# Expert blocks of 32 rows in quarter rows instead of 64 rows in half rows, in a fused encoder layer with a two-level mixture of experts

## What is computed

```python
g_sel = jnp.argmax(g_logits, axis=-1)                 # 1 of 4 groups
top_v, top_j = lax.top_k(e_logits, TOP_K)             # 2 of its 8 experts
gates = p_g[:, None] * jax.nn.softmax(top_v, axis=-1)
expert_idx = g_sel[:, None] * EXPERTS_PER_GROUP + top_j
...
def expert_block(args):
    x_b, e = args
    hid = jax.nn.silu(x_b @ w_gate[e]) * (x_b @ w_up[e])   # 1024 -> 512
    return hid @ w_down[e]                                 # 512 -> 1024
...
y = jnp.einsum('tkd,tk->td', y_assign, gates)
x = x + y ; final RMSNorm
```

## Time and profile before

| | us |
|---|---|
| device time, median of 3 runs | 866.73 |
| the 3 runs | 861.77, 866.73, 867.14 |
| the profiled execution, from its first to its last instruction (span) | 864.3 |
| PE busy in it | 831.4 (96%) |
| DVE / ACT / POOL busy | 418.5 / 215.9 / 140.0 |
| bytes moved by DMA | 261.95 MB, 303 GB/s over the span |

### The profile page before, as it was taken

One profiled execution on the slowest core, in us unless ns is written; L12 is line 12 of the kernel. 1 busy time (PEld: TensorE's weight loads), 2 busy tenths in 40 slices (PEclk: granted clock), 3 DMA queues, 4 the chain that ended last, 5 costly groups with the idle time before them and its releaser, 6 DMA issues.

```text
span 864.3 us, 15988 instructions
## 1 busy us (share of the span) xinstructions
PE 831.4 (96%) x5906; PEld 563.8 (65%) x5907; DVE 418.5 (48%) x825; ACT 215.9 (25%) x461; POOL 140.0 (16%) x279
## 2 busy tenths in 40 slices
PE   7999999999999999799999999999999999999995
PEld 5888988777877888665555555555555555555541
DVE  4699999986564535563222222222222222222237
ACT  3423211557875333101110011110111101111013
POOL 3300010000000011112222212222122222122101
PEclk9999999999999999899999999999999999999999
DMA  7353645131253198889999999999999999999998
GB/s 198 79 137 101 184 180 178 58 87 36 75 166 128 69 412 314 349 345 406 420 417 418 377 405 419 417 421 418 420 418 420 422 419 420 420 419 421 419 387 322
DMA packets 81143, 261.95 MB, mean 303 GB/s; under 512 B 19274, under 2 KB 45130, under 8 KB 56523
## 3 DMA queue, kind: packets, MB, share of 16 engines
q1 hardware_dynamic: 63392, 240.92, 71.3%
q0 software_dynamic: 7888, 18.78, 5.6%
q10 hardware_dynamic: 9818, 1.66, 1.0%
HBM read 246.49 MB, written 24.20 MB: 313 GB/s over the span
## 4 chain that ended last, share of the span: by engine, by line
PE 81%; DVE 12%; DMA 3%; issue 2%; SPq 1%; ACT 1%; POOL 0%; POOLq 0%; DVEq 0%; ACTq 0%
PE ps L1490 30%; PE ps L1536 16%; PE ps L1214 9%; PE ps L1350 8%; DVE big L1968 7%; PE ps L1504 3%; PE ps L1428 3%; PE ps L1266 2%; PE ps L1233 2%; DMA big<-results 2%; PE ps L1245 1%; PE ps L1493 1%; DVE w_split L1905 1%; DMA big<-h_rows,idx_of 1%; PE ps L1173 1%
## 5 line engine op out<-in xcount | busy, mean ns | idle before, releaser
L1493 PE MATMUL ps<-ring,big 128*64 128x256 f32 x688 | 153.9, 382 | 0.2 <-DMA ring<-in_w_up 0.2
L1490 PE MATMUL ps<-ring,big 128*64 128x256 f32 x672 | 150.3, 382 | 1.2 <-issue 1.2
L1214 PE MATMUL ps<-hT,w_split 128*128 128x256 f32 (+1 forms) x744 | 136.9, 341 | 0.0
L1490 PEld LDWEIGHTS ps<-ring,big 128*64 128x64 f32 x672 | 92.5, 138 | 56.7 <-issue 13.5
L1830 ACT ACTIVATE big<-ps 64x256 f32<-64x256 f32 x78 | 29.3, 376 | 392.5 <-PE ps L1493 341.6
L1214 PEld LDWEIGHTS ps<-hT,w_split 128*128 128x128 f32 x744 | 113.5, 190 | 20.5 <-issue 7.0
L2301 DVE TENSOR_TENSOR big<-ps,big 64x256 f32<-64x256 f32 x78 | 33.2, 426 | 182.5 <-ACT big L1830 155.1
L1490 PE MATMUL ps<-big 128*64 128x256 f32 x544 | 120.2, 379 | 0.0
L1493 PE MATMUL ps<-big 128*64 128x256 f32 x544 | 120.2, 379 | 0.0
L1490 PEld LDWEIGHTS ps<-big 128*64 128x64 f32 x544 | 74.5, 137 | 46.5 <-issue 9.7
L1493 PEld LDWEIGHTS ps<-ring,big 128*64 128x64 f32 x688 | 94.7, 138 | 1.7 <-DMA ring<-in_w_up 0.7
(11 more groups left out here) (298 smaller groups left out, 1197.4 us busy)
## 6 DMA issues: line engine op xcount, KB each, us to landing
ring<-in_w_down SPq DMA_DIRECT2D x44, 1024.0 KB
ring<-in_w_up SPq DMA_DIRECT2D x43, 1024.0 KB, 15.1
ring<-in_w_gate SPq DMA_DIRECT2D x42, 1024.0 KB
big<-in_w_gate SPq DMA_DIRECT2D x20, 1024.0 KB, 7.2
big<-in_w_up SPq DMA_DIRECT2D x20, 1024.0 KB
big<-in_w_down SPq DMA_DIRECT2D x20, 1024.0 KB
w_raw<-in_w_in SPq DMA_DIRECT2D x20, 512.0 KB, 3.8
results<-spare POOLq DMA_DIRECT2D x12, 512.0 KB, 3.3
```

Source lines behind the costliest of these rows:

```text
L1214: mm = pe.matmul(ps[:, n % 2, 0:size], w_split[:, sub, hi_w, k, :], hT[:, k // 4, hi_h, k % 4, cols], **flags)
L1490: pe.matmul(ps[0:BLK, 6 * h, 0:FH], xT[:, k, q, :], gate[2][:, k, fs], **flags)
L1493: mm = pe.matmul(ps[BLK:2 * BLK, 6 * h + 1, 0:FH], xT[:, k, q, :], up[2][:, k, fs], **flags)
```

## The change

`BLK` becomes 32 and a token row is kept as four quarter rows of 256 (`QS` = 4), so that a block of 32 tokens again fills 128 partitions. The scratch tensors have four rows for each token, and the indices sent to the indirect DMAs count quarter rows. A token's one-hot has 32 columns, so that four products (instead of two) put it on the four quarters of the partitions. `MAXN` becomes 24 and `NB` 82, and the buffers of a block are packed anew.

On PE, `gate_up` still makes two passes over the hidden columns (h), but a pass has four column groups of 32: two for gate and two for up, each with 128 moving columns. All four write one PSUM bank. Down has four groups of 32 with 256 columns each. The transposes become products with parts of the identity, 64 moving columns for the rows and 32 for the hidden halves, and `turn_hidden(b, 1)` moves behind the first quarter of down (k = 0). The last block's result, two quarters for each partition half, is scattered into half rows by DVE before `late` uses it. The loads of weights, their pieces, their waits and the table `PLACES` stay as they are.

```diff
-BLK = 64
+BLK = 32
+QS = P // BLK
...
-    h_rows = nc.dram_tensor("h_rows", (2 * T, D // 2), F32, kind="Internal").ap()
-    results = nc.dram_tensor("results", (4 * T, D // 2), F32, kind="Internal").ap()
+    h_rows = nc.dram_tensor("h_rows", (QS * T, D // QS), F32, kind="Internal").ap()
+    results = nc.dram_tensor("results", (2 * QS * T, D // QS), F32, kind="Internal").ap()
...
             def turn_rows(rows=xb):
                 for k in range(KD // 2):
-                    mm = pe.transpose(ps[:, 4, k * P:(k + 1) * P], rows[:, k:HD:KD // 2], ident[:])
+                    for e in range(2):
+                        mm = pe.matmul(ps[64 * e:64 * e + 64, 4, 2 * BLK * k:2 * BLK * (k + 1)], rows[:, k:QD:KD // 2],
+                                       ident[:].rearrange("p (q e n) -> p e q n", q=2, e=2)[:, e], start=True, stop=True)
...
-                    for half in range(2):
-                        mm = pe.matmul(ps[half * BLK:(half + 1) * BLK, 3, 0:NB], row_hot[:, a, :], block_hot[:, a, :],
+                    for s in range(QS):
+                        mm = pe.matmul(ps[s * BLK:(s + 1) * BLK, 3, 0:NB], row_hot[:, a, :], block_hot[:, a, :],
                                        start=(a == 0), stop=(a == 2 * NT - 1))
...
                 for k in range(KD // 2):
                     flags = dict(start=(q == 0 and k == 0), stop=(q == 1 and k == KD // 2 - 1))
-                    if h == 0 and k == 0:
-                        pe.wait_ge(gate[0], gate[1])
-                    pe.matmul(ps[0:BLK, 6 * h, 0:FH], xT[:, k, q, :], gate[2][:, k, fs], **flags)
-                    if h == 0 and k == 0:
-                        pe.wait_ge(up[0], up[1])
-                    mm = pe.matmul(ps[BLK:2 * BLK, 6 * h + 1, 0:FH], xT[:, k, q, :], up[2][:, k, fs], **flags)
+                    for a, (landed, target, w) in enumerate((gate, up)):
+                        if h == 0 and k == 0:
+                            pe.wait_ge(landed, target)
+                        for c in range(2):
+                            at, cols = (2 * a + c) * BLK, (2 * h + c) * P
+                            mm = pe.matmul(ps[at:at + BLK, 6 * h, 0:P], xT[:, k, q, :], w[:, k, cols:cols + P], **flags)
...
                 for k in range(KF // 2):
-                    mm = pe.transpose(ps[:, 5 * (1 - h), k * BLK:(k + 1) * BLK],
-                                      hb[:, h * FH + k:(h + 1) * FH:2], ident[0:BLK, 0:BLK])
+                    for c in range(2):
+                        mm = pe.matmul(ps[64 * c:64 * c + 64, 5 * (1 - h), k * BLK:(k + 1) * BLK],
+                                       hb[:, h * P + k:(h + 1) * P:2], ident[0:2 * BLK, c * BLK:(c + 1) * BLK], start=True, stop=True)
...
                 turn_rows()
-                turn_hidden(b, 1)
...
-                    pe.matmul(ps[0:BLK, 2, :], hbT[:, k, :], down_w[s][:, k, 0:512], start=(k == 0), stop=(k == KF - 1))
-                    mm = pe.matmul(ps[BLK:2 * BLK, 2, :], hbT[:, k, :], down_w[s][:, k, 512:1024],
-                                   start=(k == 0), stop=(k == KF - 1))
+                    if k == 1:
+                        turn_hidden(b, 1)
+                    for c in range(QS):
+                        mm = pe.matmul(ps[c * BLK:(c + 1) * BLK, 2, 0:QD], hbT[:, k, :], down_w[s][:, k, c * QD:(c + 1) * QD],
+                                       start=(k == 0), stop=(k == KF - 1))
...
-                    nc.scalar.activation(sG[:, h * FH:(h + 1) * FH], ps[0:BLK, 6 * h, 0:FH], ACT.Silu).then_inc(sg_ready[h], 1)
+                    nc.scalar.activation(sG[:, h * P:(h + 1) * P], ps[0:2 * BLK, 6 * h, 0:P], ACT.Silu).then_inc(sg_ready[h], 1)
...
-                nc.vector.tensor_tensor(hb[:, fs], ps[BLK:2 * BLK, 6 * h + 1, 0:FH], sG[:, fs],
+                nc.vector.tensor_tensor(hb[:, fs], ps[2 * BLK:4 * BLK, 6 * h, 0:P], sG[:, fs],
                                         ALU.mult).then_inc(hb_ready[h], 1)
...
-            result(last, 1, pairs + 2, late_y)
+            dve.wait_ge(base_ready, last + 1)
+            dve.wait_ge(y_done, last + 1)
+            V.scalar_tensor_tensor(late_rows[:, 0:QD], ps[:, 2, 0:QD], late_scales[:, 0, 0:1], late_rows[:, 0:QD], ALU.mult, ALU.add)
+            V.scalar_tensor_tensor(late_rows[:, QD:2 * QD], ps[:, 2, 0:QD], late_scales[:, 1, 0:1], late_rows[:, QD:2 * QD],
+                                   ALU.mult, ALU.add).then_inc(late_y, 1)
```

More of the change, by code:

```diff
@@ L1472, in rows_and_gates @@
                 for a in range(2 * NT):
-                    for half in range(2):
-                        pe.matmul(ps[half * BLK:(half + 1) * BLK, 5, 0:NB], row_hot[:, a, :], gates_block[:, a, :],
+                    for s in range(QS):
+                        pe.matmul(ps[s * BLK:(s + 1) * BLK, 5, 0:NB], row_hot[:, a, :], gates_block[:, a, :],
                                   start=(a == 0), stop=(a == 2 * NT - 1))
@@ L1477, in rows_and_gates @@
                 for t in range(NT):
[L1478 to L1479 removed]
+                    for s in range(QS):
+                        mm = pe.matmul(ps[s * BLK:(s + 1) * BLK, 5, NB:2 * NB], row_hot[:, t, :], root_block[:, t, :],
                                        start=(t == 0), stop=(t == NT - 1))
@@ L1577, in late @@
                 for half in range(2):
-                    own = slice(half * BLK, (half + 1) * BLK)
-                    mm = pe.matmul(ps[:, LATE_BANK[t] + half, :], late_hot[own, t, :], yb2[1][own, :], start=True, stop=last)
+                    own = slice(half * P // 2, (half + 1) * P // 2)
+                    mm = pe.matmul(ps[:, LATE_BANK[t] + half, :], late_hot[own, t, :], late_rows[own, :], start=True, stop=last)
                 return mm
@@ L2306, in hidden, with result @@
                     hidden_half(b, h)
-            def result(b, q, stored, evacuated=y_evac):
+            def result(b, q, stored):
                 dve.wait_ge(base_ready, b + 1)
```

110 lines of the change are left out of this document (65 added, 45 removed).

## The result

| | before | after |
|---|---|---|
| device time, median us | 866.93 (4 runs, 861.77 to 868.34) | 922.59 (4 runs, 918.3 to 923.09) |
| span of the profiled execution, us | 864.3 | 920.5 |
| PE busy, us | 831.4 | 837.1 |

The ratio is 1.0645, with a 95% interval of 1.0607 to 1.0682: 6.5% slower, outside the forecast range of 868 to 899. The direction was right, the size was not: 16.6 us were forecast and 56 came.

A forecast was written before the change was run, and what follows sets the result against it. PE and DMA were both taken as bounds. With PE late, the last weights were to land at 852.6, 16.6 us later than before; added to the median of 866.7 that gave 883.3 us, range 868 to 899.

The forecast's parts named there:

- the two bounds 3 us apart: In the kernel before, PE's chain of blocks and the DMA queue of weights both bind, ending within 3 us of each other.
- The frame of the sum: Late PE: last weights land at 500.2 + 47 P + 22 B, plus 0.6, so 852.6; the tail of 28.3 follows.
- P: PE's time for one block of 32 tokens after the change: 6.97 us, bounds 6.1 and 7.4.
- B: PE's uncovered step from one expert to the next, with two table loads: about 1.1 us, bounds 0 and 1.5.
- some 5 us sooner: At the start of the blocks, block 0 runs this much sooner, so its six pieces are issued by 374.7 us.
- a sign of being wrong: Ahead of 366 us, before the expert blocks: the span growing there by more than 1 us; about 0.4 was expected.
- 16 products for the rows at 0.029: PE's turn of the next block's rows, priced at 0.46 us a block within P.
- the sequencer is held until the second hidden half is ready: At an expert's end, PE's sequencer then has only the last 8 short groups, 0.86 us, to cover its 2.0 us.
- its cover: The first four down products hide the second hidden turn's wait; without them the next late thing costs about 0.3 us.
- The idle stretch near 390 us: DMA engines idle from 387.5 to about 395 us, until block 2 releases its slots: 7.6 us lost.
- Rows in quarters: Half as large pieces on the software DMA queue cost 0 to 9 us more; 3 us taken.
- rival 3: Four column groups on PE don't run at once, so P is 12.0 and the time about 1,145 us; chance 0.02.

The follow-up runs named there:

- runs 6 and 7: The kernel before with the turn of the next block's rows issued twice (881.81 us, ratio 1.0174), and with one of its four transposes (865.67 us, ratio 0.9988).
- run 5: The changed kernel without any load of weights after the first three slots and the lent pieces are filled: 895.63 us, ratio 1.033.
- runs 11 and 14: The changed kernel with the row turn's 64 stationary columns side by side instead of every fourth one, on two chips: 938.25 and 941.4 us.
- run 1: The changed kernel with most of the turn of the next block's rows left out (k = 0 only): 888.09 us, ratio 1.0268.
- run 2: The changed kernel with the second hidden turn back ahead of down: 909.2 us, ratio 1.0508.
- run 3: The changed kernel reading the first block from the table once per loop turn, adding the count for the other two experts: 915.85 us, ratio 1.0567.
- runs 1 to 5, 8 to 10 and 16 to 18: The changed kernel itself or with edits to row turn, hidden turn, table reads, loop places, late weights or result stores: from 883.39 to 922.12 us.

## Why the prediction was wrong in size

- **The bound before** and the two bounds 3 us apart: right, by runs 6 and 7.
- **The frame of the sum** (landing = end of place 1 + blocks x P + steps x B + the last 36 pieces + a tail of 28.3) was right: from the end of place 23 at 797.8 to the last weights are 94.2 us, where the formula has 94.4 with the measured P, and the tail is 28.5. Three terms put into it were not. The landing was to be at 852.6 and was at 892.0, 39.4 later.
- **The failed step, first part: a term that is missing.** The chain from block 0 on priced PE's instructions and not their arrival. The code of a block doubled in products, and late code cost up to 20.6 us (against run 5): 7.3 ahead of the end of place 1 (404.6 measured, 397.3 in run 5 without weights), 13.3 after it. The forecast had place 1 end at 399.1, so 5.5 of the miss lie there. Against run 5 that figure is 1.8 us too late, and so it hid a part of the error by luck; the prediction's own 391.2 + 6.97 give 398.2, and the other 0.9 has no source in it. Nor did block 0 end "some 5 us sooner": it ended 2.5 sooner, as it started 1.1 later (367.15 against 366.01, just over what the prediction named as a sign of being wrong) and its gate/up took 6.2 us, at a granted clock of 0.50 in 365 to 370 us and 0.77 in 370 to 375. No row of the kernel before warns of late code: its gap of 1.18 us between the row numbers and block 1 has no fetch in the 13 us ahead of it.
- **The failed step, second part: P was 7.34, not 6.97.** Gate/up, 3.50 us of products (32 x 0.109) against 3.58, down 1.72 as forecast, and the change of shape 0.13 each against 0.15 were right. The sizing "16 products for the rows at 0.029" was wrong: they start in pairs 0.12 us apart, 0.060 a product, 0.96 us instead of 0.46. The 0.029 came from the earlier trace rows, products of the same shape whose stationary columns stand side by side; here they stand four apart, and runs 11 and 14 show that this is the difference. The right row stood in the earlier trace rows: the transposes of 128 x 128 with the same spread columns start 0.12 apart (four in 0.72 with a change of shape). All in all 0.37 x 47 = 17.4 us. The mechanism, PE's period, was right by run 1.
- **Third: B was 1.26 on average, not 1.1.** The mechanism, "the sequencer is held until the second hidden half is ready", is shown by run 2, and the reading of the table by run 3. In the loop two ends of three cost 1.19; the third, where the loop turns, has a second branch and costs 1.59, which I didn't count. 3.5 us.
- 5.5 + 13.3 + 17.4 + 3.5 is 39.7, against the 39.4.
- **The cost of the move.** I priced the second hidden turn's new place at a change of shape of 0.15, and its cover at 0.3. It was 0.14 and, by run 2, 13 us for the kernel in all; the cover was not needed, since with the turn back in its place no wait for DVE or ACT shows from 500 to 780 us. At the new place it was the loads of down that waited for ACT, 0.2 us a block.
- **The idle stretch near 390 us** was forecast as 7.6 us from 387.5 and is 12, because block 2 starts at 397.3 instead of 391.2: the late code again.
- **Rows in quarters** were taken at 3 us. From 500 to 860 us the software queue takes 6.7% of 360 x 16 us for 9.13 MB, 42.3 ns a kilobyte, as before: nothing. So no run shows the 3 us, nor the 0.6 of them in the sum.
- **Four groups overlap** (against rival 3): four products of 128 columns start 0.007 us apart and the next four 0.109 after them (read at 578.6 us).

## What to carry to other kernels

A bound that doesn't change (here 192 pieces of 1 MiB) caps what any cut of the other bound can give; ask first what the halved unit does to the number of units (39 to 62) and to what is paid once for each, such as turns of rows, changes of shape and reading a table. Count instructions as well as their time: twice the instructions per block is twice the code, and code that is run for the first time while DMA is full can arrive late. The sequencer's lead is a resource of its own: a wait moved nearer to the end of a loop body takes it away, and whatever the sequencer does between two loops is then exposed. A product's price is to be taken from a row with the same spacing of its stationary columns, not only the same shape.

## What the runs showed of the hardware that was not expected

- Code fetched beside full DMA queues delays PE by up to 3.24 us at a time (8 of 17 fetches by 0.5 us or more); the same fetches on nearly idle engines delay it by nothing that shows inside a block (run 5).
- Once the loop over three places has run once, no more code is fetched until it is left: queue q8, which had 17 packets from 360 to 500 us, has none from 500 to 860 us in the changed kernel, and two from 860 to 892 us, for the places behind the loop.
- Stationary columns that stand four elements apart load in 213 ns where 64 side by side take 137; a pair of products then starts each 0.12 us instead of 0.06 (runs 11 and 14).
- The same kernel has two levels, 922 and 964 us, each on chips of its own, with the kernel before at 866 on all. The upper one has a pause of 0.4 us in PE's short products in nearly each block, at the time of POOL's indirect DMA. Its cause is open. The forecast is compared with the lower level, on which the first measurement and runs 1 to 5, 8 to 10 and 16 to 18 lie.
- PE's clock fell with the gaps: the granted clock was 0.80 in 380 to 390 us, with 46% of PE's time idle, 0.86 in 390 to 400 and 0.76 in 455 to 460, behind the gap of 3.24 us, part of the time at the lower of the two levels (1.2 GHz). It was 1.00 throughout from 500 to 860 us, and in run 5, without these gaps, from 370 us on to 500.
